# Encoder layer on one core: the down-projection by seven block products, with one sum of weight blocks formed in memory

## The reference, cut to what matters

```python
h = rms_norm(x, norm_ffn_pre) * (1.0 + sc2) + sh2
u = h @ w_up                                    # 2048 -> 2 * 5632
u = conv(u, conv_w, width 3 over tokens) + conv_b
a, b = split(u, 2)
y = (gelu(a) * b) @ w_down                      # 5632 -> 2048
x = x + g2 * rms_norm(y, norm_ffn_post)
```

## Time and profile before

| | |
|---|---|
| three runs | 2450.37, 2450.76, 2452.41 us (median 2450.76) |
| profiled execution | 2451.68 us, its span 2449.9 us |
| PE busy | 2366.0 us (97%), 13877 matmuls |
| DVE busy | 1697.8 us (69%) |
| ACT busy | 1021.4 us (42%) |
| transfers issued by SP | 335.14 MB, 43.5% of 16 engines' span |
| transfers issued by POOL | 25.54 MB, 2.8% |
| granted clock of TensorE | 0.99 over the span, 1.00 in the stages below |

### The profile page before, as it was taken

The page is one execution under the profiler, slowest core; times in us unless marked ns, Lnnn a source line. Parts: engine busy times, 40 slices in busy tenths (PEclk is TensorE's granted clock), DMA queues, the critical chain, the costliest instruction groups (busy, mean ns, idle before and its releaser), DMA issues.

```text
span 2449.9 us, 37360 instructions
## 1 busy us (share of the span) xinstructions
PE 2366.0 (97%) x13877; PEld 2079.3 (85%) x13877; DVE 1697.8 (69%) x2116; ACT 1021.4 (42%) x1343; POOL 60.4 (2%) x119
## 2 busy tenths in 40 slices
PE   2899999999999999989999999999999999999998
PEld 2777778888888878868999999999999988888886
DVE  6965767787777753377899999999999943334334
ACT  5356743333333432354444444444444432233322
POOL 1010000000000000000000000000000000000000
PEclk9899999999999999989999999999999999999999
DMA  9942456666555525244444344333344354423423
GB/s 371 332 140 77 134 162 190 190 206 195 185 181 184 169 69 192 78 140 141 117 120 120 116 118 120 117 116 116 118 119 121 93 182 142 149 98 112 167 94 112
DMA packets 352648, 361.63 MB, mean 148 GB/s; under 512 B 12508, under 2 KB 289252, under 8 KB 350272
## 3 DMA queue, kind: packets, MB, share of 16 engines
q1 hardware_dynamic: 345552, 335.14, 43.5%
q0 software_dynamic: 7024, 25.54, 2.8%
HBM read 338.07 MB, written 19.94 MB: 146 GB/s over the span
## 4 chain that ended last, share of the span: by engine, by line
PE 91%; DVE 3%; ACT 2%; DMA 2%; issue 1%; SPq 0%; DVEq 0%; ACTq 0%
PE bank L1810 27%; PE bank L1812 27%; PE bank L1811 27%; PE bank L1967 2%; DMA ADA<-in_w_ada_dram 1%; PE bank L1876 1%; PE bank L1999 1%; DVE ACC L1204 1%; PE bank L1986 1%; PE bank L1867 1%; PE bank L2029 1%; DMA AB_raw<-in_w_ada_dram 0%; DVE X L1768 0%; PE bank L1805 0%; PE bank L2124 0%
## 5 line engine op out<-in xcount | busy, mean ns | idle before, releaser
L1810 PE MATMUL bank<-H_lo,W_hi 128*128 128x256 f32 (+1 forms) x1888 | 660.5, 350 | 3.3 <-DVE H_lo L1219 3.3
L1812 PE MATMUL bank<-H_hi,W_lo 128*128 128x256 f32 (+1 forms) x1888 | 635.9, 337 | 0.0
L1811 PE MATMUL bank<-H_hi,W_hi 128*128 128x256 f32 (+1 forms) x1888 | 635.8, 337 | 0.0
L1810 PEld LDWEIGHTS bank<-H_lo,W_hi 128*128 128x128 f32 x1888 | 360.3, 191 | 42.8 <-issue 7.7
L1811 PEld LDWEIGHTS bank<-H_hi,W_hi 128*128 128x128 f32 x1888 | 360.4, 191 | 39.5 <-issue 7.7
L1812 PEld LDWEIGHTS bank<-H_hi,W_lo 128*128 128x128 f32 x1888 | 359.8, 191 | 37.9
L1158 DVE TENSOR_TENSOR W_lo<-W_raw,W_hi 128x1024 fp32r<-128x1024 f32 x226 | 276.1, 1222 | 133.7 <-ACT W_hi L635 123.9
L1811 PE MATMUL bank<-MGR,W_hi 128*128 128x256 f32 x1280 | 362.3, 283 | 0.0
L1812 PE MATMUL bank<-MGR,W_lo 128*128 128x256 f32 x1280 | 362.3, 283 | 0.0
L1810 PE MATMUL bank<-T_lo,W_hi 128*128 128x256 f32 x1280 | 362.3, 283 | 0.0
L635 ACT ACTIVATE W_hi<-W_raw 128x1024 fp32r<-128x1024 f32 x226 | 236.7, 1048 | 111.7 <-PE bank L1812 45.7
(11 more groups left out here) (248 smaller groups left out, 3040.8 us busy)
## 6 DMA issues: line engine op xcount, KB each, us to landing
AB_raw<-in_w_ada_dram SPq DMA_DIRECT2D x128, 512.0 KB, 4.4
UB<-in_w_up_dram SPq DMA_DIRECT2D x100, 512.0 KB, 4.1
W_raw<-in_w_in_dram SPq DMA_DIRECT2D x90, 512.0 KB, 4.5
W_raw<-in_w_down_dram SPq DMA_DIRECT2D x88, 512.0 KB, 3.6
W_raw<-in_w_up_dram SPq DMA_DIRECT2D x56, 512.0 KB, 4.0
ADA<-in_w_ada_dram SPq DMA_DIRECT2D x32, 512.0 KB, 5.8
W_raw<-in_w_out_dram SPq DMA_DIRECT2D x32, 512.0 KB, 3.8
ADA<-in_w_ada_dram SPq DMA_DIRECT2D x16, 768.0 KB, 15.5
```

Source lines behind the costliest of these rows:

```text
L1810: pe.matmul(acc, st_hi, mv_lo, start=start, stop=False)
L1811: pe.matmul(acc, st_hi, mv_hi, start=False, stop=False)
L1812: return pe.matmul(acc, st_lo, mv_hi, start=False, stop=stop)
```

## The change

The down-projection is made of couples of ff tiles (22). Of a couple, G is a 2 x 2 of blocks (two token halves of 256, two ff tiles) and w_down a 2 x 2 of blocks (two ff tiles, two column halves of 1024). The eight block products become seven. A unit is now one product of one couple: 128 x 256 of G against 128 x 1024 of weights, four banks, 12 matmuls.

- The seven products run in four sweeps over the couples: (1, 5), (6), (3, 7), (2, 4). In a sweep of two products these alternate, one set of four banks for each. 44 + 22 + 44 + 44 = 154 units.
- G blocks: product 5 needs a difference, 6 two sums, 3 a difference (DVE, `down_sums`, 256 columns, in place over G from product 6 on).
- Weight blocks: the second product of a couple takes the sum of its own raw unit and the first one's (DVE, 128 x 1024 in float32). Product 6 takes a sum of three blocks, T2, and product 4 takes T2 plus the unit of product 2.
- T2 lies in a new tensor in memory, `t2_dram`. POOL copies the first of the three blocks memory to memory, 22 transfers of 512 KB, in front of its wait for `gate_rows`, three behind each recurrent head's last unit; and adds the other two by 44 transfers with `accum_op=add`, one behind each `store_g` of the up stage.
- Raw weights: four buffers `DRAW` (two of them the old `W_raw`), each released by the low part of the couple's second unit. Unit order is swapped at the start (units 0 and 1 both of product 1) and at the end.
- G comes back by couples (512 KB) in the first sweep alone.
- At the end of each sweep ACT copies the four finished banks to SBUF (`keep`): M1, M5, M6, M3, M7. DVE combines them in the sweep behind (`middle_step`, `last_step`: 4 and 10 instructions of 1024 columns, one every four units), for the right column half with its squares (`early_squares`) and gates too. The left half gets one more sum from SBUF per bank at the end (`last_sums`).
- `X1` is loaded in the last sweep. The unit lists of SP, ACT and DVE are written out; PE keeps loops.

The diff, cut:

```diff
+COUPLES = FT // 2
+SWEEPS = ((1, 5), (6,), (3, 7), (2, 4))
+DOWN = [(s, m, e) for s, products in enumerate(SWEEPS) for m in range(COUPLES) for e in range(len(products))]
+DOWN[1], DOWN[2] = DOWN[2], DOWN[1]
+DOWN[-3], DOWN[-2] = DOWN[-2], DOWN[-3]
...
+            def load_down(d):
+                s, m, e = DOWN[d]
+                product = SWEEPS[s][e]
+                if d < 2:
+                    sp.wait_ge(lo_ready, U_DOWN - PRODUCTS + 3)
+                    sp.wait_ge(sum_ready, 2 * (FT - PLAIN) - 1)
+                elif d < SLOTS:
+                    sp.wait_ge(lo_ready, U_DOWN - 1)
+                else:
+                    sp.wait_ge(lo_ready, U_DOWN + partner(d - SLOTS) + 1)
+                if product in (6, 4):
+                    sp.wait_ge(t2_landed, 16 * 3 * COUPLES)
+                    src = t2_dram[m]
+                else:
+                    row, half = {1: (0, 0), 5: (0, 1), 3: (1, 1), 7: (0, 1), 2: (1, 0)}[product]
+                    src = w_down[0, (2 * m + row) * P:(2 * m + row + 1) * P, half * 1024:(half + 1) * 1024]
+                sp.dma_start(DRAW[d % SLOTS], src).then_inc(down_raw(d)[0], 16)
...
+            load_g(0)
+            load_g(1)
+            for d in range(len(DOWN)):
+                load_down(d)
+                s, m, e = DOWN[d]
+                if s == 0 and e == 1 and m + 2 < COUPLES:
+                    sp.wait_ge(unit_used, U_DOWN - 4 if m < 2 else U_DOWN)
...
+                    sp.wait_ge(gs_hi, DOWN.index((0, m, 0)) + 1)
+                    load_g(m + 2)
...
             pool.dma_start(MASK[:, :, :], k_masks).then_inc(masks_landed, 16)
+            for m in range(COUPLES):
+                if m % 3 == 0:
+                    pool.wait_ge(unit_used, U_HG + 10 * (m // 3 + 1))
+                pool.dma_start(t2_dram[m], w_down[0, 2 * m * P:(2 * m + 1) * P, 0:1024]).then_inc(t2_landed, 16)
             pool.wait_ge(gate_rows, 1)
...
+            def add_t2(n):
+                m, row = n % COUPLES, n // COUPLES
+                if m == 0:
+                    pool.wait_ge(t2_landed, 16 * COUPLES * (row + 1))
+                pool.dma_start(t2_dram[m], w_down[0, (2 * m + row) * P:(2 * m + row + 1) * P, 1024:2048],
+                               accum_op=ALU.add).then_inc(t2_landed, 16)
             for j in range(FT):
                 store_g(j)
+                add_t2(j)
...
+            def down_hi(d):
...
+                    act.wait_ge(unit_used, U_DOWN + d - SLOTS + 1)
...
+                act.activation(GS_hi[:, d % SLOTS, :], down_moving(d), ACT.Copy).then_inc(gs_hi, 1)
+                if e == 1:
+                    act.wait_ge(sum_ready, 2 * (FT - PLAIN) + W_SUMS[d + 1])
+                else:
+                    act.wait_ge(*down_raw(d))
...
+                act.activation(W_hi[:, (U_DOWN + d) % SLOTS, :], DRAW[d % SLOTS], ACT.Copy).then_inc(hi_ready, 1)
...
+                if d == SWEEP_AT[1] + 1:
+                    for n in range(4):
+                        keep(SWEEP_AT[1] - 2, y_M1, 4, n)
...
+            def down_sums(d):
+                s, m, e = DOWN[d]
+                product, n = SWEEPS[s][e], 4 + G_SUMS[d]
+                if e == 1:
+                    first = DOWN.index((s, m, 0))
+                    dve.wait_ge(*down_raw(first))
+                    dve.wait_ge(*down_raw(d))
+                    dve.tensor_tensor(DRAW[d % SLOTS], DRAW[d % SLOTS], DRAW[first % SLOTS], ALU.add).then_inc(sum_ready, 1)
+                a11, a12, a21, a22 = [g_block(m, tok, k) for tok in range(2) for k in range(2)]
+                if product == 5:
...
+                    dve.tensor_tensor(GT[:, m % 2, :], a22, a21, ALU.subtract).then_inc(t_sums, 1)
+                elif product == 6:
+                    dve.tensor_tensor(a21, a11, a21, ALU.subtract).then_inc(t_sums, 1)
+                    dve.wait_ge(t_sums, n + 1)
+                    dve.tensor_tensor(a11, a21, a22, ALU.add).then_inc(t_sums, 1)
+                elif product == 3:
+                    dve.tensor_tensor(a11, a11, a12, ALU.subtract).then_inc(t_sums, 1)
...
+            def last_sums(tt, banks):
+                dve.wait_ge(y_tile_done, tt + 1)
+                dve.wait_ge(posted, POSTED_LAST)
+                for b in banks:
+                    if b == 7:
+                        dve.wait_ge(unit_used, U_END)
+                    dve.tensor_tensor(PB[b][:, :], PB[b][:, :], YG[:, tt, b % 2 * 512:(b % 2 + 1) * 512], ALU.add).then_inc(posted, 1)
...
                     else:
-                        g_low(0, 0, p + LEAD - PRODUCTS)
-                        split_lo(0, 4, U_DOWN + p + LEAD - PRODUCTS)
+                        if p == PRODUCTS - 1:
+                            down_sums(2)
+                        down_low(p + LEAD - PRODUCTS)
...
+            down_low(2)
+            down_sums(3)
+            for d in range(3, len(DOWN)):
+                if d + 1 < len(DOWN):
+                    down_sums(d + 1)
+                down_low(d)
+                if d == 4:
+                    glu(FT - 1, 1)
+                for n in range(4):
+                    if d == SWEEP_AT[2] + 4 * n + 4:
+                        middle_step(n)
+                for n in range(len(Y_STEPS)):
+                    if d == SWEEP_AT[3] + 4 * n + 4:
+                        last_step(n)
             for tt in range(TT):
+                banks = (6,) if tt == TT - 1 else (2 * tt, 2 * tt + 1)
+                last_sums(tt, banks)
+                gate_y(tt, banks)
+                if tt == TT - 1:
+                    last_sums(tt, (7,))
...
+            def down_unit(d, c, bank0, first, last, order=range(4)):
+                down_ready(d)
+                for b in order:
+                    bank = bank0 + b
...
+                    ins = down_bank(c, b, bank, first, last)
                 ins.then_inc(unit_used, 1)
...
+            d0 = len(DOWN) - 4
+            for tt in range(TT - 1):
+                for d in (d0 + 2 * (tt // 2), d0 + 2 * (tt // 2) + 1):
+                    down_ready(d)
+                    for b in (2 * (tt % 2), 2 * (tt % 2) + 1):
+                        ins = down_bank(d % 4, b, b + 4 * (tt // 2), False, d % 2 == 1)
                 ins.then_inc(y_tile_done, 1)
```

More of the change, by code:

```diff
@@ L87 @@
 NOT_RAW = PRODUCTS * (FT - PLAIN) // 2
-U_END = U_DOWN + 2 * FT
+COUPLES = FT // 2
[3 more added lines that the diff above has]
+DOWN[-3], DOWN[-2] = DOWN[-2], DOWN[-3]
+SWEEP_AT = [0, 2 * COUPLES, 3 * COUPLES, 5 * COUPLES]
+W_SUMS = [sum(1 for s, m, e in DOWN[:d] if e == 1) for d in range(len(DOWN) + 1)]
+G_SUMS = [sum({5: 1, 6: 2, 3: 1}.get(SWEEPS[s][e], 0) for s, m, e in DOWN[:d]) for d in range(len(DOWN) + 1)]
+U_END = U_DOWN + len(DOWN) - 2
 V_BADA = 0
@@ L1100, in down_squares, with early_squares, last_squares @@
+            def early_squares(tt):
+                act.wait_ge(posted, Y_POSTED[tt])
+                for c in range(2):
+                    if 2 * tt + c >= 1:
+                        act.wait_ge(y_squared, 2 * tt + c)
+                    act.activation(JY[:, :], YG[:, tt, 1024 + c * 512:1024 + (c + 1) * 512], ACT.Square,
+                                   accum_out=col(SM, SSY + tt * 4 + 2 + c)).then_inc(y_squared, 1)
+            def last_squares(tt):
                 for b in (2 * tt, 2 * tt + 1):
-                    if p == 1 and b == 7:
-                        act.wait_ge(unit_used, U_DOWN + 2 * FT)
-                    else:
-                        act.wait_ge(yg_ready, 8 * p + b + 1)
@@ L2198, in _ @@
                         product(i, jj, p)
[L2201 to L2208, removed]
-                        pe.wait_ge(conv_r, 2 * FT - 2)
-                    if first and p == 0 and b == 2:
-                        pe.wait_ge(posted, 7 * (FT - PLAIN))
-                    if first and p == 0 and b < 2:
-                        pe.wait_ge(conv_r, 2 * FT - 1 + b)
-                    if first and p == 1:
-                        pe.wait_ge(yg_ready, b + 1)
-                        pe.wait_ge(y_squared, b + 1)
-                    ins = down_bank(k, b, first, False)
-                ins.then_inc(unit_used, 1)
@@ L2242, in _, with down_bank @@
-            for p in range(2):
-                for k in range(4):
-                    down_unit(p, 0, k)
-                with pe.Fori(1, FT // 4 - 1) as i:
-                    for k in range(4):
-                        down_unit(p, i, k)
-                down_last_units(p)
+            def down_bank(c, b, bank, first, last):
+                slot = (U_DOWN + c) % SLOTS
+                t, w = slice(b // 2 * P, (b // 2 + 1) * P), slice((b % 2) * 512, (b % 2 + 1) * 512)
+                return three_passes(PB[bank][:, :], GS_hi[:, c, t], GS_lo[:, c, t], W_hi[:, slot, w], W_lo[:, slot, w], first, last)
@@ new lines, in _ @@
+            for d in range(2):
+                down_unit(d, d, 4, d == 0, False)
+            for d in range(2, 4):
+                down_unit(d, d, 0, d == 2, False, (2, 3, 0, 1))
```

(23 more changed lines are left out.)

255 lines of the change are left out of this document (136 added, 119 removed).

## The result

Four runs of the changed kernel took 2425.6 to 2431.2 us, median 2428.7, against 2450.4 to 2455.3, median 2451.6, of the kernel before on the same chips: ratio 0.990, 95% interval 0.989 to 0.992, so 22.9 us faster. The forecast was 37 us faster, 2414.5 us. The measured median lies inside the range of 2400 to 2442, but outside the band of 2407 to 2423 that was given 57%. The profiled execution took 2431.2 us, the longest of the four.

The account below looks back on a forecast made before the run. PE's matmuls were taken to bound the down stage. From the profiled 2451.7 us: -60.0 -0.9 +1 +9 +12.6 +1 +1 = -36.3, 2415.4; the median, 0.9 lower, 2414.5 us. Range 2400 to 2442.

Parts of the forecast that it names:

- Removed matmuls, -60.0: Down stage: 264 matmuls fewer at 0.2273 us each, -60.0 us if PE stays fed.
- The wait between the old column passes: Down stage: PE's wait where DVE gated finished banks goes, as ACT now copies them: -0.9 us.
- The start, +9: Start of the down stage: PE waits before units 2, 3 and 4, 7.3 us together, plus 1.7 for the broadcast; bounds 2 and 18.
- The wait beside the broadcast: Start of the down stage: 1.7 us added because the 1 MB gate-row broadcast is released among the next loads.
- The load loop, +1: Paired sweeps: raw-buffer loop of 10.3 us fits under PE's 10.9 per two couples; +1 us for odd late loads, bounds 0 and +36.
- L: Paired sweeps: time from buffer release to both raw loads landed, taken at 4.7 us, in the first sweep 5.8.
- The rival on the load loop: Paired sweeps: L of 6.8 us makes loads set the pace, +13 us over 33 rounds, start recovers no lead: 2432 us; 20%.
- the prediction's own signs: If right: PE gaps of 7 to 11 us before unit 5, almost none after; loads landing in 4 to 6 us.
- X1, +1: Last sweep: X1's 4 MB meet loads of twice the rate, one couple's loads perhaps late: +1 us, bounds 0 to 4.
- The tail, +12.6: End: from PE's end to the span's end 22.0 us instead of 9.4, with 1.2 us more DVE sums per tile; bounds 9 and 16.
- Memory sums, +1: T2 transfers: copies at recurrent heads cost +1 us in all, adding transfers in the up stage 0.
- The Trainium skill's rule on descriptors: Certain DVE operations keep GpSimd from writing descriptors: fivefold transfer time, 21 us estimated per 4.2 us transfer; given no time.

Follow-up runs that it names:

- early release: Changed kernel, a couple's first raw buffer released by its own unit's low part (units 0, 1: by the weight sum reading them): 2417.7 us, ratio to before 0.986.
- the G load behind: Changed kernel, G load of couple m+2 issued once G of couple m has landed, right behind a couple's two raw loads: 2420.3 us, ratio to before 0.988.

## Why the prediction was right, and where it was wrong

**Removed matmuls, -60.0: right.** 1848 matmuls, three passes 0.68 us apart where PE is fed. The wait between the old column passes is gone too.

**The start, +9: the waits in the right places, the collision mis-sized.** The waits before units 2, 3 and 4 were 0.5, 1.2 and 4.2 us (forecast 2.2, 0.3 and 4.8), 5.8 together for 7.3 worked out, and early release took most of the last one. The wait beside the broadcast, put at 1.7 us, was 6.1: the raw loads issued at 1978.4 and 1978.8 landed after 9.8 and 13.3 us, beside the broadcast, the last adding transfer and a G load. I had counted the collision with the broadcast only. The wait was 2.35 us with the broadcast moved, 4.2 without adding transfers, 2.8 with the G load behind, 4.5 with early release; in the run that changed only the tail it was 5.1, so two executions that are alike up to there differ by 1 us.

**The load loop, +1: this is the step that failed**, by its size, L. "Two in flight I take at 4.7, and in the first sweep [...] 5.8": measured 3.6 and 6.7 to 7.0. From the release to both landed it is a little more than one landing, because the second load is issued behind the first: L was 7.4 to 8.2 us there, and with DVE's 4.6 (forecast 4.5) the loop is 12.1 to 12.8 us against PE's 10.9. It cost 6.3 us of waits in the first sweep, 5 more than forecast. I had the G load in L's bytes but not its place: it waits for ACT's copy, and so stands directly ahead of the next pair in the same queue. The rival on the load loop was right about the mechanism in one sweep of three; the other paired sweeps never waited for their loads but beside X1. Its time, 2432, is nearer to the measured one than the forecast, but by luck: it charged 13 us to 33 rounds, where 11 rounds cost 6, and the rest came from the start and the clock. By the prediction's own signs, gaps "almost none after" unit 5 and loads landing in 4 to 6 us did not hold; 14 us of waits stand behind unit 5.

**Not in the sum: the clock.** Behind three of the waits (4.2, 6.1, 2.4 us) the granted clock was at its lower level, 1.2 of 2.4 GHz. Windows behind those waits (PE, PEclk, DMA share, GB/s):

```profile
1976.40:1979.60 3.20, 3.16 (x8) 0.51 0.66 218
1995.30:2000.00 4.70, 4.70 (x11) 0.50 0.62 180
2082.30:2085.80 3.50, 3.50 (x9) 0.51 0.58 177
```

11.4 us at half rate are 5.7 us, so these three waits cost 1.4 to 1.7 times their own length.

**X1, +1: 1.8.** One wait, at 2336.2 us. With spread loads and early release 0.4 was left of it, but early release without spreading left 1.1 and 0.3 (with the broadcast moved), so what spreading does is not shown.

**The tail, +12.6: right.** 22.2 us behind the last matmul for 22.0, with its 1.2 us a tile (6.53 - 5.33).

**Memory sums, +1: 0.** PE is busy 693.24 us of 350 to 1060 before and 693.43 after, and the up stage kept its length. The Trainium skill's rule on descriptors ("SBUF — State Buffer", see the prediction) made no difference to the time here: the adding transfers landed in 7.8 us and the G stores in 4.0 (medians), far from the 21 us of that estimate; the longest landing was 10.2 us, beside other transfers. The rule names certain DVE operations, and no run here tells whether this stage's are among them.

In sum, the profiled execution was 15.8 us above the forecast for it: load loop +5.3, broadcast +4.4, clock +5.7, X1 +0.8, less 1.5 before unit 5 at the start and 1 for the copies, which leaves 2 for the restart of PE behind its waits (0.1 us each) and what is not assigned.

## What to carry to other kernels

When PE's work per unit is halved, the buffers ahead of it last half as long: work out the loop from release to landing to split as a time, with every transfer of its queue in its real place, and not as a share of bandwidth. Release each buffer at its own last reader, and issue what has time to spare behind what has none. Look at large transfers that are "only once": where they meet others at a start without lead, loads of 512 KB took 13 us here instead of 4, though moving the one broadcast alone gained nothing that the medians show. A wait can cost more than its length: behind three of the ten waits the clock was at half.

## What the runs showed of the hardware that was not expected

- An accumulating transfer of 512 KB from memory to memory landed in 5.8 to 10.2 us, median 7.8, and 44 of them left the up stage's length as it was. They do slow the loads beside them. Four loads into UB, issued from about 1155 to 1168 us, landed after 8.9, 7.0, 5.4 and 4.7 us without adding transfers, after 11.1, 9.5, 7.6 and 6.8 with one beside them (the changed kernel), and after 13.7, 11.9, 10.1 and 9.5 with two in a row. Only two in a row made PE wait, 2.1 us: the slack ahead of PE covered the rest.
- The drop of the clock is not a fixed price: 1.8 us of waiting at 2336.2 us was followed by none, 2.35 at 2082.3 by 3.5 us of it, and 2.35 at 1992.0 in another kernel by none.
